# Attention in a two-layer hybrid backbone: maxima made in pairs of row groups, row sums added up on GpSimd over all key tiles and turned by one-column products

## The reference, cut to what matters

```python
def diff_attend(q, k, v, lam):
    s = jnp.einsum('bqhmd,bkhmd->bhmqk', q, k).astype(F32) * (DA_QK ** -0.5)
    p = jax.nn.softmax(s, axis=-1)
    w = p[:, :, 0] - lam * p[:, :, 1]
    return jnp.einsum('bhqk,bkhv->bqhv', w, v)
```

## Time and profile before

| | before |
|---|---|
| median of 3 runs | 7675.96 us |
| the profiled execution | 7679.03 us |
| its span, first to last instruction | 7677.4 us |
| TensorE busy | 6178.2 us (80%) |
| VectorE busy | 3287.9 us (43%) |
| ScalarE busy | 1687.4 us (22%) |
| GpSimd busy | 1440.2 us (19%) |
| mean granted TensorE clock | 0.896 |

### The profile page before, as it was taken

The page is one execution under the profiler, slowest core; times in us unless marked ns, Lnnn a source line. Parts: engine busy times, 40 slices in busy tenths (PEclk is TensorE's granted clock), DMA queues, the critical chain, the costliest instruction groups (busy, mean ns, idle before and its releaser), DMA issues. The chain is left out here.

```text
span 7677.4 us, 80199 instructions
## 1 busy us (share of the span) xinstructions
PE 6178.2 (80%) x28400; PEld 3330.2 (43%) x28436; DVE 3287.9 (43%) x5327; ACT 1687.4 (22%) x4077; POOL 1440.2 (19%) x1351
## 2 busy tenths in 40 slices
PE   8499999832578699999869999996228887999989
PEld 8244444421466533333334444443126664333334
DVE  0122222258566655553212333323866566555522
ACT  0011111110233323334101111111003332333331
POOL 0000000012333224344000000000223331344330
PEclk9999999955799889999989999997559996999999
DMA  3611111134322200000341111111442211000012
GB/s 132 127 47 45 45 46 48 41 104 126 112 83 75 67 16 6 1 6 5 119 170 47 45 46 48 45 41 60 132 135 75 86 65 50 1 6 6 4 74 91
DMA packets 306663, 475.60 MB, mean 62 GB/s; under 512 B 124812, under 2 KB 177372, under 8 KB 299460
## 3 DMA queue, kind: packets, MB, share of 16 engines
q1 hardware_dynamic: 275556, 397.24, 16.0%
q10 hardware_dynamic: 25632, 55.62, 1.9%
q0 software_dynamic: 5184, 18.88, 0.8%
HBM read 313.81 MB, written 157.54 MB: 61 GB/s over the span
## 5 line engine op out<-in xcount | busy, mean ns | idle before, releaser
L411 PE MATMUL psum<-projection_W,projection_hT 128*128 128x512 f32 (+2 forms) x5760 | 2277.2, 558 | 52.6 <-DVE projection_hT L503 52.6
L411 PEld LDWEIGHTS psum<-projection_W,projection_hT 128*128 128x128 f32 x5760 | 1104.3, 192 | 1204.8 <-issue 1157.0
L2073 PE MATMUL psum<-attention_QK 32*128 32x512 f32 (+1 forms) x2592 | 934.9, 634 | 50.2 <-DVE attention_mxp L1952 41.4
L1952 DVE TENSOR_REDUCE attention_mxp<-psum 128x1 f32<-128x512 f32 (+1 forms) x1136 | 688.0, 632 | 587.5 <-PE psum L2073 585.5
L1884 POOL TENSOR_TENSOR attention_PP<-attention_PT 128x512 f32<-128x512 f32 (+1 forms) x584 | 719.1, 1263 | 1105.6 <-ACT attention_PT L2030 968.0
L2030 ACT ACTIVATE attention_PT<-psum 128x512 f32<-128x512 f32 (+1 forms) x1168 | 606.0, 598 | 1161.9 <-PE psum L2128 1161.6
L520 DVE TENSOR_SCALAR projection_e<-projection_e 128x256 f32<-128x256 f32 (+1 forms) x180 | 57.6, 320 | 1499.7 <-ACT projection_e L467 1499.7
L2073 PEld LDWEIGHTS psum<-attention_QK 32*128 32x128 f32 x2592 | 341.9, 197 | 538.7 <-DVE attention_mxp L1952 206.6
L2140 PE MATMUL psum<-attention_PT,attention_va 128*64 128x512 f32 x2336 | 572.7, 612 | 0.0
L460 ACT ACTIVATE projection_ut<-psum 128x512 f32<-128x512 f32 (+1 forms) x360 | 150.1, 427 | 1771.9 <-PE psum L411 1771.9
L2127 PE MATMUL psum<-attention_QK 32*128 32x512 f32 x2336 | 497.9, 634 | 11.9 <-ACT attention_MT L2019 11.9
(11 more groups left out here) (321 smaller groups left out, 6788.7 us busy)
## 6 DMA issues: line engine op xcount, KB each, us to landing
u<-projection_ut SPq DMA_DIRECT2D x252, 256.0 KB, 2.0
states_x<-xbc SPq DMA_DIRECT2D x108, 384.0 KB, 4.6
projection_W<-in_w_in SPq DMA_DIRECT2D x16, 2316.0 KB, 28.5
mixing_hg<-u SPq DMA_DIRECT2D x36, 1024.0 KB, 5.0
modulation_wm<-in_w_mod SPq DMA_DIRECT2D x12, 2048.0 KB, 7.7
output_y<-y SPq DMA_DIRECT2D x34, 512.0 KB, 4.5
xbc<-projection_ut SPq DMA_DIRECT2D x36, 384.0 KB, 2.3
xc<-states_xc ACTq DMA_DIRECT2D x36, 384.0 KB, 2.3
```

Source lines behind the costliest of these rows:

```text
L411: ins = nc.tensor.matmul(ps[n % RING][:, 0:w], hT[b][:, q], W[:, q, c0:c0 + w], start=(q == 0), stop=(q == KT - 1))
L1952: ins = V.tensor_reduce(mxp[:, q, r, a:a + 1], bk[job][:, 0:hi - lo], AX.X, ALU.max)
L2073: return T(out[:, 0:hi - lo], QK[rows(r), a0, t * P:(t + 1) * P], QK[rows(r), 2 + a0, lo:hi], start=True, stop=True)
```

## The change

Maxima: a job now makes a pair of products, of row groups 0 and 1 or 2 and 3, in banks 6 and 7 together. TensorE waits for both banks and then issues both products; VectorE reduces both. For the last, narrow chunk of 256 keys a job has two query tiles side by side in a bank. A half has 36 jobs with 72 reductions, one ahead of `values` and the others behind it.

Row sums: the jobs `sum`, the buffers `PP` and `Srow` and VectorE's additions are gone. GpSimd adds every step's `PT` to the running sum `SA`, two instructions for each step from the second on, each over two row groups (1024 elements). `sm` waits for the last of these and makes the sums over the keys with sixteen one-column products (`SA` slice as weights, one column of ones). ScalarE's wait before it overwrites `PT` is for GpSimd's additions of four steps before.

```diff
-            todo = [("mx", x + 1, q, a, r) for q in range(nq) for a in range(len(chunks)) for r in range(RG)]
+            todo = maxima_of(x + 1)
             for i in range(n):
                 part = todo[len(todo) * i // n:len(todo) * (i + 1) // n]
-                before[first[x] + i] += part[:2]
-                after[first[x] + i] += part[2:]
+                before[first[x] + i] += part[:1]
+                after[first[x] + i] += part[1:]
...
+    def maxima_of(x):
+        nq, chunks = groups[halves[x][0]][1], groups[halves[x][0]][3]
+        wide = [(q, 1, a) for q in range(nq) for a, (lo, hi) in enumerate(chunks) if hi - lo > 256]
+        narrow = [(q, 2, a) for q in range(0, nq, 2) for a, (lo, hi) in enumerate(chunks) if hi - lo <= 256]
+        return [("mx", x, *j, pr) for j in wide + narrow for pr in range(2)]
...
-                    if i % 2 and i < len(steps):
...
-                            ins = G.tensor_tensor(PP[m % 2][:, r, 0:w], PT[(i - 1) % PTB][:, r, 0:w], PT[i % PTB][:, r, 0:w],
-                                                  ALU.add)
-                        ins.then_inc(s["pp_done"], 1)
+                    if i < len(steps) and steps[i][1]:
...
+                            if n > 1:
+                                gp.wait_ge(s["added"], added[i - 1] - 1 + pr)
+                            one = PT[(i - 1) % PTB] if n == 1 else SA[x % 2]
+                            G.tensor_tensor(SA[x % 2][:, rs, 0:w], one[:, rs, 0:w], PT[i % PTB][:, rs, 0:w], ALU.add) \
+                                .then_inc(s["added"], 1)
...
-                            act.wait_ge(s["pp_done"], (i - PTB) // 2 + 1)
+                            act.wait_ge(s["added"], added[i - PTB])
...
-                        bk.take(pe, job)
-                        ins = scored(bk[job], x, *job[2:])
-                    if kind == "sum":
-                        m = first[x] // 2 + job[2]
-                        pe.wait_ge(s["pp_done"], m + 1)
-                        bk.take(pe, job)
-                        for r in range(RG):
-                            ins = T(bk[job][rows(r), 0:w], ones[:], PP[m % 2][:, r, 0:w], start=True, stop=True)
+                        q, nn, a, pr = job[2:]
+                        lo, hi = groups[halves[x][0]][3][a]
+                        for j in range(2):
+                            bk.take(pe, (job, j))
+                        for j in range(2):
+                            for i in range(nn):
+                                ins = scored(bk[job, j], x, q + i, a, 2 * pr + j, i * (hi - lo))
+                            bk.done(ins, (job, j))
+                        return
                     if kind == "sm":
-                        bk.freed(pe, ("sum", x, (last[x] - first[x] + 1) // 2 - 1))
+                        pe.wait_ge(s["added"], added[last[x]])
                         bk.take(pe, job)
                         for q in range(nq):
-                            ins = nc.tensor.transpose(bk[job][:, q * P:(q + 1) * P], Srow[x % 2][:, q * P:(q + 1) * P], k.ident[:])
+                            for r in range(RG):
+                                ins = T(bk[job][:, q * RG + r:q * RG + r + 1], SA[x % 2][:, r, q * P:(q + 1) * P], ones[:, 0:1],
+                                        start=True, stop=True)
```

More of the change, by code:

```diff
@@ L1754, in attention @@
     after = [[] for _ in range(SLOTS)]
-    for x in range(len(halves)):
-        for m in range((last[x] - first[x] + 1) // 2):
-            after[first[x] + 2 * m + 3].append(("sum", x, m))
+    def maxima_of(x):
[3 more added lines that the diff above has]
+        return [("mx", x, *j, pr) for j in wide + narrow for pr in range(2)]
     for x in range(len(halves)):
@@ L1762, in attention @@
         if x + 1 < len(halves):
-            nq, chunks = groups[halves[x + 1][0]][1], groups[halves[x + 1][0]][3]
-            todo = [("mx", x + 1, q, a, r) for q in range(nq) for a in range(len(chunks)) for r in range(RG)]
+            todo = maxima_of(x + 1)
             for i in range(n):
                 part = todo[len(todo) * i // n:len(todo) * (i + 1) // n]
-                before[first[x] + i] += part[:2]
-                after[first[x] + i] += part[2:]
+                before[first[x] + i] += part[:1]
+                after[first[x] + i] += part[1:]
             after[last[x]].append(("turn", x + 1))
     ring = [("turn", 0)] + [j for i in range(SLOTS) for j in before[i] + after[i]]
-    uses = [(j, 6 + n % 2) for n, j in enumerate(ring)]
+    uses = []
+    for j in ring:
+        if j[0] == "mx":
+            uses += [((j, 0), 6), ((j, 1), 7)]
+        else:
+            uses.append((j, 7 if j[0] == "sm" or j[0] == "ot" and j[2] else 6))
     uses += [(("st", i, r), r) for i in range(len(steps)) for r in range(RG)]
+    added = [2 * (i - x + (n == 0)) for i, (x, n) in enumerate(steps)]
     finish = {last[2 * g + 1] + 5: g for g in range(NG)}
@@ L1785, in attention @@
         PT = [k.sb(c, f"PT{b}", [P, RG, QG * P]) for b in range(PTB)]
-        PP = two("PP", [P, RG, QG * P])
+        SA = two("SA", [P, RG, QG * P])
         mxp = k.sb(c, "mxp", [P, QG, RG, 5])
@@ L1873, in _ @@
                 for i in range(SLOTS):
-                    if i % 2 and i < len(steps):
-                        m = i // 2
-                        x = steps[i][0]
+                    if i < len(steps) and steps[i][1]:
+                        x, n = steps[i]
                         w = groups[halves[x][0]][1] * P
-                        for r in range(RG):
[L1879 to L1883, removed]
-                            ins = G.tensor_tensor(PP[m % 2][:, r, 0:w], PT[(i - 1) % PTB][:, r, 0:w], PT[i % PTB][:, r, 0:w],
-                                                  ALU.add)
-                        ins.then_inc(s["pp_done"], 1)
+                        for pr in range(2):
+                            rs = slice(2 * pr, 2 * pr + 2)
+                            for r in (2 * pr, 2 * pr + 1):
+                                if n == 1:
+                                    bk.freed(gp, ("st", i - 1, r))
+                                bk.freed(gp, ("st", i, r))
+                            if n == 1 and x >= 2:
+                                bk.wait(gp, ("sm", x - 2))
+                            if n > 1:
[3 more added lines that the diff above has]
+                                .then_inc(s["added"], 1)
                     if i - 2 in finish:
@@ L1990, in _ @@
                         x = steps[i + 1][0]
-                        for job in [j for j in before[i] + after[i] if j[0] == "mx"][-2:]:
-                            bk.freed(dve, job)
+                        for job in [j for j in before[i] + after[i] if j[0] == "mx"][-1:]:
+                            for j in range(2):
+                                bk.freed(dve, (job, j))
                         maxima(x + 1)
@@ L2072, in scored @@
                     t = t0 + q
-                    return T(out[:, 0:hi - lo], QK[rows(r), a0, t * P:(t + 1) * P], QK[rows(r), 2 + a0, lo:hi], start=True, stop=True)
+                    return T(out[:, at:at + hi - lo], QK[rows(r), a0, t * P:(t + 1) * P], QK[rows(r), 2 + a0, lo:hi],
+                             start=True, stop=True)
                 pe.wait_ge(s["key_copied"], NT)
```

32 lines of the change are left out of this document (14 added, 18 removed).

## The result

| | before | after |
|---|---|---|
| median | 7675.14 us (7672.12 to 7679.13) | 7746.74 us (7731.98 to 7757.92) |
| the profiled execution | 7679.03 us | 7742.2 us |
| its span | 7677.4 us | 7740.5 us |
| mean granted TensorE clock | 0.896 | 0.873 |

The changed kernel is slower: the ratio is 1.0092, with a 95% interval of 1.0073 to 1.011. (Both medians are of four runs each.) The forecast of 7641 us had the wrong sign, and 7747 lies above the range of 7555 to 7705.

The account below looks back on a forecast made before the run. It took a ring of waits between maxima products and VectorE's reductions as the bound, TensorE setting the pace. Halves -98, clock +39, last halves +16 and +8 gave -35 us: 7644, as median 7641 us, range 7555 to 7705.

Parts of the forecast that it names:

- The plain step: Attention step with two jobs: pair waits for both banks, is issued at once; 5.42 us, 13 of them in a half.
- The end-of-half work: Sixteen one-column products replace four transposes: 3.65 us of products, 10.7 us for the step with `sm`, 7.0 with second `ot`.
- slot 8, third pair: First of a half's two steps with three jobs: the third waits 2.51 us more for the second's reductions; 7.9 us.
- The price of a one-column product: In `sm` at a half's end: 0.114 us a record, taken from mixing; upper end 0.215, from modulation.
- Rival 4: One-column products cost 0.215 us a record: 7685 us; chance 0.14 together with the clock's upper bound.
- The chain: At a half's end, two small VectorE links each wait for one GpSimd addition: 4.1 us stall in each of 14 turns.
- TensorE's clock: Near-empty stretches around `sm` (12) and before next scores (14): two in three cost 3.0 us at half clock; +39 net.
- Rival 2: Half-clock stretches behind the 26 gaps take the gain, so slower; two stretches a gap give 7746 us; chance 0.12.
- Rival 1: Stalls before the turn don't come, no more half-clock stretches than now: 7533 us, 7587 with half of each; chance 0.27.
- The last halves: GpSimd's additions bind each layer's last half: +16 us in layer 1, +8 in layer 0, whose context halves hide part.
- GpSimd in the regular halves: Halves with maxima: 34 additions, 81 us of GpSimd, under the half's 111.6 us, so nothing was counted.
- Rival 3: GpSimd binds in every half, from 3.19 us an addition upwards; 7759 us at 3.3; chance 0.05.

Follow-up runs that it names:

- The first two experiments: Two runs, ratios to the kernel before: paired maxima with the old row sums, 7802.63 us (1.0154); GpSimd's row sums with single maxima, 7685.98 us (1.0004).
- the run with all fillers: Kernel after plus thrown-away products ahead of the turn, among the one-column products and ahead of a third pair of maxima: 7690.25 us, ratio 1.0008 to before.
- the best version: Kernel after with last-step additions behind the maxima chain, wide-product sums, last halves' additions on VectorE, thrown-away products ahead of third pairs: 7513.61 us, 0.9778 of before.

## Why the prediction was wrong, point by point

**The plain step** was right: 5.52 against 5.42 us, 1.3 for a half. The first two experiments show too that it needs both parts of the change.

**The end-of-half work** was right in size at the full clock, which the run with all fillers shows:

| term | forecast | at the full clock | in after, one half |
|---|---|---|---|
| 13 plain steps | 70.5 | 71.8 | 73.3 |
| slot 2, `sm` | 10.7 | 10.3 (14.16 - 3.84) | 14.2 |
| slot 3, second `ot` | 7.0 | 7.2 | 8.9 |
| slot 8, third pair | 7.9 | 8.1 | 8.1 |
| slot 16, third pair | 6.3 | 6.6 | 8.6 |
| slot 17, chain and turn | 9.2 | 9.1 | 9.7 |
| a half | 111.6 | 113.0 | 122.9 |

**The price of a one-column product** was put as a choice between two rows, 0.114 and 0.215 us a record. Here it was both: 0.101 to 0.112 at the full clock and 0.208 (added records) or 6.99 / 32 = 0.218 (end of layer 1) at half clock. In layer 0 of after, where the clock fell among them, they came 0.144 us apart in the mean. Taking the cheaper row asked for a condition, the clock at that place, which I didn't name. Rival 4 had the size of it, but not as a matter of the clock.

**The chain** was right in mechanism and size. Two links wait for one addition each, and slot 17 takes 9.05 us at the full clock against 5.09 in the best version, so the stall is 4.0 us where 4.1 was forecast. In after TensorE itself is slow there and shows only 1.5 us of it as a wait.

**TensorE's clock is the step that failed.** I gave 17 of 26 places 3.0 us each, 51 us, less 12 for the stretches that were there. The twelve middle halves add up to 20.2 us more than before; 12 x (113.0 - 118.6) - 12 = -79 of that is the work, so half clock costs about 99 us in the profiled execution, by this estimate (95 with 113.4), twice the term. Two things were wrong. The third pair's gap of 1.46 us was not on the list of places at all, and two such gaps stand in each half. And a place doesn't have one price. Where the sums were made harmless, the stretch came at slots 8 and 9 instead, and a stretch that begins in the one-column products goes on into the next step (slot 3, 8.94 instead of 7.15 us). Rival 2 described this and had 0.12, and the row against it (scores and values bring the clock back) was read from a kernel without such gaps. That its 7746 us for two stretches a gap is the measured time is luck: it had 156 us for the clock, where about 99 were lost, and 24 us for the ends, where 53 were. (Rival 1's first number takes off all 51 us of new stretches and still counts -12 for the old ones; with as many as now it would be 7545, not 7533.)

What the earlier trace rows said in its favour, TensorE busy without a gap and at 0.50, was the most telling row of the whole set, and I had it as an argument for a rival alone. The Trainium skill, "TensorE: Matmul & The Clock Gate", section "HAM oscillation — how this bites in real kernels", ties the loss to waits that come back each time round a loop. As I read that rule, all 26 places pay, which gave +27 us on my sum. The traces agree for the waits ahead of the turn: products in that gap kept the clock at 1.00 behind it. They show half clock around the third pair too, behind waits of 1.46 us, and without any wait, in the one-column products.

**The last halves** were forecast at +16 and +8 us and came to +21.9 and +31.0 (20.1 and 10.8 for the last half of layer 0 and the context halves). In layer 1 the wait for GpSimd is 15.2 us, nearly as forecast, and the one-column products behind it run at half clock, 3.3 us more. In layer 0 I had taken it that the short context halves hide most of GpSimd's remainder. Instead the cast of the next half's maxima took 22.11 us, to the end of GpSimd's 30 additions, and TensorE waited for the turn. I had let each link wait for one addition, as in the earlier trace rows. Here some nine additions followed each other without a gap on GpSimd, and the cast ended only with the last of them. With the additions on VectorE it took 0.18 us, so they are what held it; why it didn't get in between two of them, no run shows.

**GpSimd in the regular halves** doesn't bind: 2354 ns an addition, 369 us idle in all. Rival 3 is refuted, as is rival 1, since the stalls came. That leaves these parts of the miss of 98 us on the profiled executions: 48 the clock, 29 the ends, 15 the plain step and smaller sizes, 6 the phases that were not changed.

## What to carry to other kernels

When a change takes work off the engine that sets the pace, look at what is left in each thin place at 5 us windows, and price the whole sum once at the full and once at the half clock. Here the work of a half was 5% less (113.0 against 118.6 us) and the time of a layer 0 half 4% more. A gap that can't be closed may be worth filling with products that do nothing, and most so when no other thin place remains: filling one of three brought nothing that can be told (the sums) or 0.5% (the turn), filling the last one 0.8%. And small instructions of VectorE that TensorE waits for belong ahead of GpSimd's long ones, by a wait on GpSimd if need be.

## What the runs showed of the hardware that I had not expected

- The clock stands at 0.50 while TensorE's products and weight loads are both busy 5.00 of 5.00 us, with one column in each product. With one product of 512 columns ahead of every eight records it stood at 1.00 over them.
- A VectorE cast of 128 x 8 elements, 0.18 us where GpSimd made no additions, took 22.11 us beside a run of GpSimd additions. It didn't get in between two of them, though one such addition lasts 2.35 us.
- The same addition of 128 x 1024 elements takes 1.22 us on VectorE and 2.35 on GpSimd.
- Adding products made kernels faster: twelve records of waste in each half of the best version brought 58 us.
